# One modulation sum moves to projection unit 14, a weight split stands behind the first heads' softmax steps, and the exponential's table is loaded ahead

## The reference, cut to what matters

```python
sh1, sc1, gt1, sh2, sc2, gt2 = ada_mod(c, w_ada[l], b_ada[l])     # silu(c) @ w_ada + b_ada, in six parts
h = modulate(rmsnorm(x, g_attn[l]), sh1, sc1)                     # h * (1 + scale) + shift
qa, ka, va, qb, kb, vb, ga, gb = project(h, w_in[l], ...)         # one product, then QK norms
ya = window_attention(qa, ka, va, cache_a_k, cache_a_v, sink_a)   # 8 heads, a sink logit in the softmax
yb = neighbourhood_attention(qb, kb, vb, cache_b_k, cache_b_v, rpb_b)
x = x + gt1 * ((sigmoid(ga) * (ya @ w_out_a) + sigmoid(gb) * (yb @ w_out_b)) @ w_o)
x = x + gt2 * swiglu(modulate(rmsnorm(x, g_ffn[l]), sh2, sc2), w_gate[l], w_up[l], w_down[l])
```

## Time and profile before

| | |
|---|---|
| median of 3 runs | 985.27 us (983.03, 985.27, 987.27) |
| the profiled execution | 988.04 us |
| its span in the trace | 986.3 us |
| PE busy | 962.7 us, 98% |
| DVE busy | 493.8 us, 50% |
| ACT busy | 356.3 us, 36% |
| POOL busy | 10.4 us, 1% |
| mean granted TensorE clock | 0.981 |

### The profile page before, as it was taken

The page is one execution under the profiler, slowest core; times in us unless marked ns, Lnnn a source line. Parts: engine busy times, 40 slices in busy tenths (PEclk is TensorE's granted clock), DMA queues, the critical chain, the costliest instruction groups (busy, mean ns, idle before and its releaser), DMA issues.

```text
span 986.3 us, 16347 instructions
## 1 busy us (share of the span) xinstructions
PE 962.7 (98%) x6613; PEld 899.0 (91%) x6613; DVE 493.8 (50%) x893; ACT 356.3 (36%) x674; POOL 10.4 (1%) x13
## 2 busy tenths in 40 slices
PE   5999999899999999999989999999999999999998
PEld 5688888677777999999979999999999999999998
DVE  3557997798688653233484333233333324233332
ACT  4563354566766522221355332111222221122220
POOL 0000000000000000000030000000000000000000
PEclk7899999899999999999989999999999999999999
DMA  9745333622244122521221322222222212222221
GB/s 369 291 175 187 137 105 124 198 87 85 101 159 149 43 79 72 192 65 64 64 64 48 103 69 80 64 86 69 81 66 83 69 59 91 80 70 80 67 81 67
DMA packets 33066, 104.23 MB, mean 106 GB/s; under 512 B 3696, under 2 KB 8944, under 8 KB 31856
## 3 DMA queue, kind: packets, MB, share of 16 engines
q1 hardware_dynamic: 32288, 102.64, 30.3%
q10 hardware_dynamic: 720, 0.77, 0.2%
HBM read 99.07 MB, written 4.33 MB: 105 GB/s over the span
## 4 chain that ended last, share of the span: by engine, by line
PE 95%; DVE 3%; ACT 1%; DMA 1%; issue 0%; ACTq 0%; DVEq 0%
PE ps L1293 65%; PE ps L1389 13%; PE ps L1592 5%; PE ps L1513 3%; PE ps L1489 3%; PE ps L1498 3%; PE ps L1342 1%; DMA x<-x_t 1%; PE ps L1413 1%; DVE scr L1225 1%; DVE scr L941 1%; PE ps L1351 0%; DVE h_lo L915 0%; DVE scr L1222 0%; PE ps L1372 0%
## 5 line engine op out<-in xcount | busy, mean ns | idle before, releaser
L555 ACT ACTIVATE w_hi<-stage 128x1024 fp32r<-128x1024 f32 x118 | 124.3, 1058 | 312.2 <-PE ps L1293 269.3
L905 DVE TENSOR_TENSOR w_lo<-stage,w_hi 128x1024 fp32r<-128x1024 f32 x116 | 142.0, 1225 | 177.8 <-ACT w_hi L555 174.9
L1293 PE MATMUL ps<-h_hi,w_hi 128*128 128x320 f32 x896 | 208.8, 314 | 0.5 <-ACT scr L655 0.4
L1293 PE MATMUL ps<-h_lo,w_hi 128*128 128x320 f32 x896 | 204.4, 309 | 0.0
L1293 PE MATMUL ps<-h_hi,w_lo 128*128 128x320 f32 x896 | 204.3, 309 | 0.0
L1293 PEld LDWEIGHTS ps<-h_hi,w_hi 128*128 128x128 f32 x896 | 148.4, 188 | 10.6 <-issue 8.7
L1293 PEld LDWEIGHTS ps<-h_lo,w_hi 128*128 128x128 f32 x896 | 150.1, 188 | 0.0
L1293 PEld LDWEIGHTS ps<-h_hi,w_lo 128*128 128x128 f32 x896 | 150.1, 188 | 0.0
L1293 PE MATMUL ps<-y_lo,w_hi 128*128 128x320 f32 x480 | 109.4, 309 | 0.0
L1293 PE MATMUL ps<-y_hi,w_hi 128*128 128x320 f32 x480 | 109.4, 309 | 0.0
L1293 PE MATMUL ps<-y_hi,w_lo 128*128 128x320 f32 x480 | 109.3, 309 | 0.0
(11 more groups left out here) (167 smaller groups left out, 1183.2 us busy)
## 6 DMA issues: line engine op xcount, KB each, us to landing
stage<-w_main SPq DMA_DIRECT2D x118, 512.0 KB, 3.5
x<-w_ada SPq DMA_DIRECT2D x23, 512.0 KB, 4.6
qk<-w_ada SPq DMA_DIRECT2D x7, 1024.0 KB, 12.1
bb<-rpb SPq DMA_DIRECT2D x16, 256.0 KB, 3.9
qk<-w_ada SPq DMA_DIRECT2D x5, 512.0 KB, 3.6
x<-x_t SPq DMA_DIRECT2D x1, 2560.0 KB, 9.4
y_t<-x SPq DMA_DIRECT2D x8, 320.0 KB, 2.2
vf<-w_ada SPq DMA_DIRECT2D x4, 512.0 KB, 3.7
```

What stands on the lines that cost most here:

```text
L555: act.activation(w_hi[:, slot, :], stage[:, slot, :], ACT.Copy).then_inc(hi_done, 1)
L905: dve.tensor_tensor(w_lo[:, slot, :], stage[:, slot, :], w_hi[:, slot, :].bitcast(F32), ALU.subtract).then_inc(lo_done, 1)
L1293: ins = pe.matmul(out[:, half, :], wt[:, w_slot, w], rt[:, rk, half * TH:(half + 1) * TH], start=start and n == 0, stop=stop and n == 2)
```

## The change

Three edits. First, the number of modulation sums at unit 17 goes from 1 to 0 and at unit 14 from 0 to 1. The sums keep their order, so that each of the numbers 11 to 15 is done a place earlier. Second, the split of unit 21 moves: its hi part from ahead of `exps(0)` to behind it, its lo part from VectorE's loop to behind `negate_scores(1)`. Third, an exponential of one number (`small[:, 52:53]`) stands ahead of `take_vb` on ScalarE.

```diff
-ADA2_OF = [0, 0, 0, 1, 2, 1, 1, 1, 1, 0, 0, 2, 2, 0, 0, 2, 2, 1]
+ADA2_OF = [0, 0, 0, 1, 2, 1, 1, 1, 1, 0, 0, 2, 2, 0, 1, 2, 2, 0]
...
+            act.activation(small[:, 52:53], eps, ACT.Exp)
             take_vb()
-            split_next(17)
...
             exps(0)
+            split_next(17)
             exps(1)
...
-                    split_lo(u + RING, u % RING)
+                    if u < N_QKV - 1:
+                        split_lo(u + RING, u % RING)
...
             negate_scores(0)
             normalise(0)
             negate_scores(1)
+            split_lo(N_QKV - 1 + RING, (N_QKV - 1) % RING)
             for p in range(N_PAIRS):
```

## The result

The changed kernel takes 978.28 us, the median of 13 runs (977.08 to 982.45); the kernel before, in 13 runs that include the three known at the prediction, takes 983.87 (982.05 to 988.96). The ratio is 0.9936, 95% interval 0.9923 to 0.9950: 6.3 us, or 0.64%, faster. The two medians lie 5.6 us apart, 0.57%, which is inside that interval. The profiled execution took 982.45 us with a span of 980.5 us, 5.8 us less than the span before.

The account below looks back on a forecast made before the run. TensorE was taken as the bound, waiting for VectorE where attention begins. Old gaps of 3.2 us less 1.3 of new ones, plus some 2.7 of half-speed work, gave 4.6 us: 985.27 - 4.6 = 980.7 us, range 978.3 to 984.0.

Parts of the forecast that it names:

- The bound: Start of attention: TensorE bounds the kernel, with two gaps, 3.2 us together, waiting for VectorE's `negate_scores`.
- The order of the first pairs: Start of attention: no idle before `scores(1)`, about 1.0 us before `scores(2)`, 0.3 before `scores(3)`; 4.6 us saved.
- The share of the clock: Half-speed TensorE stretch behind attention's 2.44 us gap: its going gives some 2.7 of the 4.6 us saved.
- the rival: Attention's half-speed stretch is not in every run before, or the new kernel has one too: 982.7 us, chance 0.24.
- The split, the sum, the table: Moved work on VectorE and ScalarE: split hidden with 0.4 us to spare, 2.4 us sum and 1.28 us load cost nothing.
- SP's queue: Attention's loads and v writes: queue 2.6 us later, slack 8.9 to 1.7 us; slower or equal by it, chance 0.04.
- The prediction's sign: VectorE's sum of modulation tile 16 waiting for its load would show the forecast wrong.
- The sum, which is the step that failed: Whole kernel: the 4.6 us saving taken off the median of three runs, 985.27, gives 980.7 us.
- The third rival: Larger saving: earlier reads of `scores(1)` and a shorter later clock dip take 1 to 2 us more, 979 us; chance 0.10.
- The chances: Whole kernel: faster by over 0.5% 0.33, within 0.5% 0.64, slower 0.03.

Follow-up runs that it names:

- e4: Kernel before with ten extra 512-column matmuls on TensorE ahead of `scores(1)`, nothing moved: 981.07 us, ratio 0.9970 to the kernel before.
- e10: Kernel before with fourteen extra 320-column matmuls (2.06 us) ahead of the last gate unit: 985.69 us, ratio 1.0013 to the kernel before.
- e1: Kernel before with only the modulation sum moved from unit 17 to unit 14: 978.46 us, ratio 0.9933 to the kernel before.
- e3: Changed kernel without the early one-number exponential, so the table loads right ahead of `exps(0)`: 978.32 us, ratio 0.9940 to the kernel before.
- e7: Changed kernel with 5 and 18 extra matmuls ahead of the sixth and seventh products of the FFN's first unit: 976.48 us, ratio 0.9911 to the kernel before.
- e9: Changed kernel with nine extra 320-column matmuls (1.3 us) ahead of the last gate unit: 979.90 us, ratio 0.9959 to the kernel before.
- e11: Changed kernel with extra matmuls both at the start and ahead of the FFN's sixth and seventh products: 974.87 us, ratio 0.9899 to the kernel before.
- e12: Changed kernel, unchanged, run again for a second trace: 977.66 us, span 975.9 us.
- e2: Kernel before with only the split of unit 21 moved on ScalarE and VectorE: 978.75 us, ratio 0.9940 to the kernel before.
- e8: Changed kernel with ten extra fp32 matmuls (4.3 us) in TensorE's idle time at the start: 977.10 us, ratio 0.9923 to the kernel before.
- e5: Kernel before, unchanged, run again for a second trace: 982.96 us.

## Why the prediction was right and where it was wrong

**The bound.** Right. Both gaps waited for VectorE, and with VectorE out of the way TensorE gained what it had lost.

**The order of the first pairs.** Right nearly to the tenth. Forecast: `scores(1)` with no idle, 1.0 us of idle ahead of `scores(2)`, the whole 4.6 us shorter. Measured: none, 1.00, and 4.76. The reciprocal of `normalise(1)` came 1.13 us behind the split's start, at 178.54 (178.1 + 0.49 forecast). The 0.3 us expected ahead of `scores(3)` shrank to less than the trace lists as a wait, and `scores(3)` came at 181.01 where 180.6 + 0.49 = 181.09 was forecast. That is 0.08 of the 0.16 us between 4.6 and 4.76; the other 0.08 is in the forecast itself, whose 185.28 - 180.6 is 4.68.

**The share of the clock.** The prediction prices the half-speed stretch twice: at 2.7 us in the split of its 4.6, which leaves 1.9 for the waits, and at 2.0 in the rival's working. e4 measured 2.2, and 2.6 for the waiting. So the parts of the 4.6 were off by 0.5 and 0.7 us in opposite directions, and the sum came out close in part by luck. The rival's premise, that the stretch is not in every run before or comes back after, was wrong: it was given 0.24. Three traces of three of the kernel before have it, and e10's, none of the changed one, nor of e1 to e3, e7 to e9, e11 or e12.
The Trainium skill (TensorE: Matmul & The Clock Gate, Part 1) has the number of slow matmuls at a kernel's start run-variable. That agrees with the start here, with stretches of 7, 10 and 20 us in traces of one kernel. The page says it of a kernel's start, and the prediction carried it over to the attention gap, where the fall came 0.5 to 0.6 us behind the gap's end in all three traces. Run-variable in one stretch was no evidence for another.

**The split, the sum, the table.** Each was costed at nothing on the path, and each was. What the prediction did not say is that the two edits on VectorE are redundant (e1, e2). It had all the numbers for it: 2.4 us for the sum, 4.8 us of lateness, and three gate steps that cover the rest. For the table the trace had 1.28 us and the next ACTIVATE 1.30 us behind the load's start, and `take_vb` still waited 0.22 us for TensorE. The 2.66 us of the Trainium skill (ScalarE: Activation LUTs, What ACT_TABLE_LOAD costs) would have pushed it back by 0.9; the trace does not agree, and the gate step's wait stayed at 0.36 us.

**SP's queue.** Right in direction, the slack was oversized, and the place where it bites first was not the one watched. Forecast: v writes landed at 189.4, `take_gate(0)` at 191.1. Measured in the first trace after:

```profile
182.41 6.53 SPq L466 DMA_DIRECT2D v_grid<-scr  x8
190.96 0.40 SPq L469 DMA_DIRECT2D vb<-v_grid  x1
```

and `take_gate(0)` at 191.47. The slack was 0.5 us and not 1.7, since the eight writes took 8.6 us from the first issue to landing where they had taken 7.5, and 0.8 of the difference is their issue (6.5 us, 5.7 before). In e12 ScalarE did wait 0.35 us there and in e3 0.4 us, with no wait on TensorE behind it. In e2, e8 and e11 the delay of this queue reached TensorE, by way of modulation tile 18, the first one that SP loads behind the reads of v, and cost 1.0, 1.4 and about 1.2 us. (The prediction's sign was a wait for tile 16; no trace shows one.) In the changed kernel's first trace tile 18 lands 0.7 us before it is used, in e12 just in time. So this rival was given 0.04 and is at work in some runs of the new order, at a size that still leaves a gain; how many of the changed kernel's own 13 runs pay it no trace shows, and its two traces don't. A further gain ahead of this place runs into the queue, as e8's did.

**The sum, which is the step that failed.** "Taking the saving off the median: 985.27 - 4.6" has two faults. The base was the middle of three runs; over 13 the kernel before is 983.87, 1.4 us lower. And the saving was that of one place, with all other places taken as unchanged: the low stretch at the FFN had no term, while the change also shifts when the FFN's gap meets the fall of the clock. In three traces of three the kernel before had the long stretch there; the changed kernel had the short one in both of its traces. That is worth 1.5 us in the first pair of traces, 0.9 in the pair e5 and e12, and 1.0 on the mean of the seven long and five short cases (472.1 us against 471.1 from the gap's end to the end of the span). Together: 980.7 - 1.4 - 0.16 = 979.1, and 978.3 was measured; the remaining 0.8 us is a difference and not a measurement, and the FFN's 0.9 to 1.5 covers it. By the mean clock some of the changed kernel's 13 runs may have had the long stretch; no trace shows one. The third rival, "the clock's later dip is also shorter in the new runs, 979 us", named the mechanism. It was given 0.10, and both traces of the changed kernel have it. It is luck all the same that this change got it: the beginning of attention is as short in e2 and e8, which have the long stretch, and 1.3 us more in e9 bring it back. The page before shows the dip at slice 21; the prediction gave no term to it. The range's lower end missed by 0.02 us, and with the base of 13 runs the same sum gives 979.3, 1.0 us above the measured time.

**The chances.** Faster by over 0.5% had 0.33 and happened, with an interval from 0.50% to 0.77%.

## What to carry to other kernels

A gap in TensorE's work costs its length and what the clock loses behind it; here 2.44 us of waiting drew 2.2 us more. In these traces a gap of 0.9 to 1.0 us ahead of `scores(2)` was followed by no fall of the clock (ten of ten), the 2.44 us with 0.7 behind it by one in four of four, and the FFN's 0.9 and 3.07 us by one in twelve of twelve. Gaps like the last two are worth breaking, by moved work or, failing that, by matmuls into a free bank. Where a kernel has several such gaps, a gain ahead of one changes what the next costs: read each low stretch of the clock and its place against its gap before taking a local saving as the whole. And take the base from as many runs as the difference needs, and compare traces whose starts are alike.

## What the runs showed of the hardware that was not expected

The low stretches come in few lengths. Over 14 traces the start has 6.8, 10.2 or 20.5 us (once 10.2, a pause of 3.4 at full speed, and 3.4), attention 6.8, the FFN 6.8 or 10.2 and, filled, 3.4 or none. At the FFN the same gap of 3.07 us gives 6.8 us where the clock falls from 0.6 us ahead of its end to 0.3 us behind it (five traces), and 10.2 us where it falls 0.9 to 1.8 us ahead (seven). The difference costs 1.0 us on the mean of these traces, with single traces from 0.4 to 1.6 us apart. A VectorE multiplication slows down beside GpSimd's copies: the pair at `normalise` over 512 columns takes 0.88 us alone, 1.7 with the copies begun 0.2 to 0.4 us behind it, and 2.3 to 2.5 where they begin with it or 0.2 us ahead. The start alone spreads the same kernel by 5 us: the mean clock of the kernel before takes the values 0.988, 0.986, 0.984 and 0.981 to 0.983, with spans from 981 to 987 us.
